# Eight experts over a shared weight stream: a smaller token form, and a scatter over whole row tiles

## The reference, cut to what matters

```python
def _swiglu(h, wg, wu, wd):
    return (jax.nn.silu(h @ wg) * (h @ wu)) @ wd

def _moe(h, router_w, router_b, wg, wu, wd):
    logits = (h @ router_w + router_b).astype(jnp.float32)
    top_v, top_i = lax.top_k(logits, MOE_TOPK)          # MOE_TOPK = 2, N_EXPERTS = 8
    top_w = jax.nn.softmax(top_v, axis=-1)
    gates = jnp.sum(top_w[..., None] * jax.nn.one_hot(top_i, N_EXPERTS, dtype=jnp.float32), axis=-2)
    out = jnp.zeros_like(h)
    for e in range(N_EXPERTS):
        out = out + gates[..., e:e + 1] * _swiglu(h, wg[e], wu[e], wd[e])
    return out
```

## Time and profile before

| | before |
|---|---|
| median of 3 runs | 2109.98 us (2108.65 to 2113.43) |
| profiled execution, its own time | 2107.95 us |
| its span | 2106.2 us |
| TensorE busy, share of the span | 1964.2 us, 93% |
| LDWEIGHTS busy | 1400.2 us, 66% |
| VectorE / ScalarE / GpSimd busy | 508.5 / 276.1 / 363.9 us |
| mean granted TensorE clock | 0.965 |
| chain of work that ended last | TensorE 83%, DMA 8%, VectorE 4% |
| read from HBM | 531.08 MB, mean 253 GB/s |
| one issue of expert weights | 1024.0 KB |
| GB/s in the 40 slices of the span, slices 21 to 40 | 307 393 392 393 351 394 394 395 394 393 394 302 240 240 280 371 395 325 187 22 |

### The profile page before, as it was taken

The page is one execution under the profiler, slowest core; times in us unless marked ns, Lnnn a source line. Parts: engine busy times, 40 slices in busy tenths (PEclk is TensorE's granted clock), DMA queues, the critical chain, the costliest instruction groups (busy, mean ns, idle before and its releaser), DMA issues.

```text
span 2106.2 us, 27964 instructions
## 1 busy us (share of the span) xinstructions
PE 1964.2 (93%) x11330; PEld 1400.2 (66%) x11331; DVE 508.5 (24%) x1165; ACT 276.1 (13%) x518; POOL 363.9 (17%) x215
## 2 busy tenths in 40 slices
PE   2999999989999999999899899998888999998998
PEld 2888788867776888888765555554435877654444
DVE  6293754110001291533220101110101100100002
ACT  1202312010001203412010001000000000101002
POOL 1706750069995000000000000000000000000000
PEclk8899999989999899999989899999999999999998
DMA  9999863268686789733589999999999866799950
GB/s 270 228 183 182 204 187 115 72 221 283 234 288 136 131 147 142 123 121 120 190 307 393 392 393 351 394 394 395 394 393 394 302 240 240 280 371 395 325 187 22
DMA packets 287088, 533.82 MB, mean 253 GB/s; under 512 B 12496, under 2 KB 125696, under 8 KB 286976
## 3 DMA queue, kind: packets, MB, share of 16 engines
q1 hardware_dynamic: 271232, 489.72, 73.6%
q0 software_dynamic: 10880, 41.95, 5.7%
q10 hardware_dynamic: 4864, 0.50, 0.2%
HBM read 531.08 MB, written 1.05 MB: 253 GB/s over the span
## 4 chain that ended last, share of the span: by engine, by line
PE 83%; DMA 8%; DVE 4%; issue 2%; ACT 2%; SPq 1%; POOL 1%; ACTq 0%; DVEq 0%
PE ps L654 20%; PE ps L988 16%; PE ps L1023 9%; PE ps L717 7%; PE ps L726 7%; PE ps L1052 6%; PE ps L737 4%; DMA ring<-in_moe_w_up 4%; PE ps L1068 3%; PE ps L947 2%; PE ps L964 2%; DMA xc<-in_moe_w_down 1%; DMA proj<-in_ada_w 1%; DMA proj<-in_moe_w_up 1%; PE ps L1008 1%
## 5 line engine op out<-in xcount | busy, mean ns | idle before, releaser
L654 PE MATMUL ps<-hT,ring 128*128 128x256 f32 x2048 | 454.6, 383 | 0.0
L654 PEld LDWEIGHTS ps<-hT,ring 128*128 128x128 f32 x2048 | 391.0, 192 | 56.1 <-issue 2.9
L988 PE MATMUL ps<-ring,proj 128*64 128x256 f32 (+2 forms) x1768 | 205.5, 369 | 15.1 <-DMA ring<-in_moe_w_gate 7.9
L567 POOL TENSOR_TENSOR aring<-aring,ccol 128x2048 f32<-128x2048 f32 x40 | 144.7, 3618 | 232.2 <-ACT hT L1163 136.6
L988 PEld LDWEIGHTS ps<-ring,proj 128*64 128x64 f32 (+2 forms) x1768 | 119.5, 133 | 94.6 <-issue 45.1
L1713 DVE TENSOR_TENSOR proj<-proj,ps 128x256 f32<-128x256 f32 (+2 forms) x49 | 23.4, 478 | 648.4 <-PE ps L988 648.4
L726 PE MATMUL ps<-hT,ring 128*128 128x256 f32 x704 | 158.9, 388 | 4.0 <-ACT hT L1163 4.0
L726 PEld LDWEIGHTS ps<-hT,ring 128*128 128x128 f32 x704 | 136.6, 195 | 23.5 <-issue 4.4
L573 POOL TENSOR_TENSOR aring<-aring 128x1024 f32<-128x1024 f32 x80 | 149.0, 1862 | 6.3
L1283 ACT ACTIVATE proj<-ps 128x256 f32<-128x256 f32 (+2 forms) x49 | 21.1, 430 | 622.9 <-PE ps L988 622.9
L1023 PE MATMUL ps<-ring,proj 128*64 128x512 f32 (+2 forms) x360 | 88.3, 608 | 7.9 <-DMA ring<-in_moe_w_down 4.9
(11 more groups left out here) (293 smaller groups left out, 2094.3 us busy)
## 6 DMA issues: line engine op xcount, KB each, us to landing
ring<-in_w_in SPq DMA_DIRECT2D x64, 1024.0 KB, 12.7
ring<-in_moe_w_up SPq DMA_DIRECT2D x56, 1024.0 KB, 14.0
ring<-in_moe_w_gate SPq DMA_DIRECT2D x48, 1024.0 KB, 14.0
aring<-in_ada_w POOLq DMA_DIRECT2D x40, 1024.0 KB, 8.7
ring<-in_moe_w_down SPq DMA_DIRECT2D x40, 1024.0 KB, 13.8
aring<-in_moe_w_gate SPq DMA_DIRECT2D x32, 1024.0 KB, 13.0
extra<-in_moe_w_up SPq DMA_DIRECT2D x16, 1024.0 KB, 14.7
proj<-in_moe_w_down SPq DMA_DIRECT2D x16, 1024.0 KB, 13.7
```

Source lines behind the costliest of these rows:

```text
L567: last = g.tensor_tensor(w, w, ccol[:, :].unsqueeze(2).broadcast_to([P, KT, 256]), ALU.mult)
L654: last = mm(ps[:, n % 2, j * SEQ:(j + 1) * SEQ], wide(s)[:, k, j * P:(j + 1) * P], hT[:, k, :], start=(k == 0), stop=(k == KT - 1))
L988: last = mm(ps[rows * c:rows * (c + 1), bank, 4 * t0:4 * (t0 + rows)], xg[:, 4 * h + k, t0:t0 + rows], w[:, k, 4 * rows * c:4 * rows * (c ...
```

## The change

- `SIZES` gets a sixth, smallest size of 32 (`QUARTER`). `token_blocks(32)` is one block of 32 tokens, which the code of the body already knows: four column tiles. E0, E3 and E6 (24, 30 and 20 tokens) now take this body; the others take the ones they took.
- `by_size` goes, `by_tiles` takes its place: one comparison, 128 or 256 rows. `scatter` uses whole row tiles of 128.
- `ysb` must then hold numbers in the rows that have no token: VectorE sets them to zero (`empty_rows`) in the step g = 1, behind the last `merge` of the expert before. It is one or two memsets of 32 or 64 partitions x 1024; none for the sizes 128 and 256.

```diff
-SIZES = (HALF, 96, 128, 160, 256)
+SIZES = (QUARTER, HALF, 96, 128, 160, 256)
...
-        def by_size(eng, count, body):
-
-            def at(i):
-                if i == len(SIZES) - 1:
-                    body(SIZES[i])
-                    return
-                with eng.If(count <= SIZES[i]):
-                    body(SIZES[i])
-                with eng.Else():
-                    at(i + 1)
-                    eng.nop()
-            at(0)
+        def by_tiles(eng, count, body):
+
+            with eng.If(count <= P):
+                body(P)
+            with eng.Else():
+                body(SEQ)
...
                     for st in range(slot_tiles):
-                        rows = min(P, n - st * P)
-                        last = mm(ps[:, 6 + (m + 1) % 2, 0:SEQ], ysb[0:rows, st, m * P:(m + 1) * P],
-                                  pgT[0:rows, st, :], start=(st == 0), stop=(st == slot_tiles - 1))
+                        last = mm(ps[:, 6 + (m + 1) % 2, 0:SEQ], ysb[:, st, m * P:(m + 1) * P], pgT[:, st, :], start=(st == 0), stop=(st == slot_tiles - 1))
...
                     pe.wait_ge(ye_s, e + 1)
-                    by_size(pe, before, lambda slots: scatter(slots, e * PER + CF0 + C1 - 1))
+                    by_tiles(pe, before, lambda slots: scatter(slots, e * PER + CF0 + C1 - 1))
...
                         if g == 1:
                             merge_before()
+                            empty_rows(n)
                             after = count_after(dve, e)
...
+                def empty_rows(n):
+                    tile, first = (n - 1) // P, (n - 1) % P + 1
+                    while first < P:
+                        rows = HALF if first == HALF else QUARTER
+                        v.memset(ysb[first:first + rows, tile, :], 0.0)
+                        first += rows
```

More of the change, by code:

```diff
@@ L1100, in prepare @@
                     pe.wait_ge(p_s, e + 2)
-                    with pe.If(after <= P):
-                        gather(e * PER + CF0 + C1 + KT, P)
-                    with pe.Else():
-                        gather(e * PER + CF0 + C1 + KT, SEQ)
+                    by_tiles(pe, after, lambda slots: gather(e * PER + CF0 + C1 + KT, slots))
                 return rows_stationary(n) if n <= P else weights_stationary(n)
@@ L1110, in _ @@
             pe.wait_ge(ye_s, EXPERTS + 1)
-            by_size(pe, last_count, lambda slots: scatter(slots, PER * EXPERTS + CF0 + C1 - 1))
+            by_tiles(pe, last_count, lambda slots: scatter(slots, PER * EXPERTS + CF0 + C1 - 1))
             norm_sums(2 * DEPTH)
@@ L1743, in prepared @@
                     v.tensor_copy(pgT[:, 0:st, :], ps[:, 6, 0:st * SEQ].rearrange("p (a b) -> p a b", a=st)).then_inc(cf_s, 1)
-                    with dve.If(after <= P):
-                        tokens(P)
-                    with dve.Else():
-                        tokens(SEQ)
+                    by_tiles(dve, after, tokens)
                 def tokens(width):
```

## The result

The changed kernel took **2117.93 us** (median of 8 runs, 2114.84 to 2119.02); the kernel before, in runs between them on the same chip, 2114.18 (8 runs, 2108.65 to 2118.02). The ratio is **1.0035, with a 95% interval of 1.0019 to 1.0050**: a little slower, where 2087 and a gain of 1% were forecast, and outside the range of 2080 to 2100. The profiled execution took 2116.28 us (before 2107.95), its span is 2114.6.

A forecast was written before the change was run, and what follows sets the result against it. The weight stream bounds up to E4's end, then TensorE through the last three experts. Terms -7 - 1.7 - 8 - 1.7 - 4.35 = -22.8 take the profiled 2107.95 to 2085.2, median 2087 us; range 2080 to 2100.

The forecast's parts named there:

- That jump costs E2 about 3.8 us by E5's row: Entry into the body for 64, no longer behind the ladder: a jump of about 3.8 us, with nothing lost.
- term E: Entry into E7's body: shifted code removes one of two pauses, -4.35 us (bounds 0 and +4.35).
- Term A: E0 to E4, up to the stream's delivery of unit 210: earlier restart and fewer stream stalls, -7 us (bounds -8 and -2).
- E1 stays near the edge: Within E0 to E4: the 67-token expert barely stops filling the slots, so -7 us was taken from 7.8.
- If E3 weren't there, the 3.8 would be on the path: Jump of 3.8 us into the body for 64: hidden because the next expert has 57 us of work in 112 us of stream.
- The sign named in the prediction: End of the 67-token expert: a stream still at 356 GB/s there would show Term A wrong.
- Terms B and D: Scatters in the 153-token expert and E7: no lower clock on down records behind them, -1.7 us each (0 to -2).
- Term C: E6: the weight stream decides instead of TensorE, ending about 1905, -8 us (bounds -4 and -10).
- At nothing: Memsets on VectorE: 1.7 us each, at most 3.4, hidden behind other work, so costed at nothing.
- Low clock: Rival: idle TensorE lowers the clock, costing the ends of E0 and E6; +7, 2094 us; chance 0.17.
- The small form starves on its own instructions: Rival: late code or half clock makes the 32-token step 12.8 us in E0 and E6; 2150 us; chance 0.05 (slower).
- Scatter only: Rival: the 32-token step is no shorter than 10.85 us, Term A and Term C fall away; 2102 us; chance 0.06.

The follow-up runs named there:

- E0: Not a run: the kernel's expert with 24 tokens; 89.4 us in the kernel before, 82.1 in the changed kernel.
- E6: Not a run: the kernel's expert with 20 tokens; 91.8 us in the kernel before, 86.4 in the changed kernel.
- E7: Not a run: the kernel's expert with 128 tokens; 169.4 us in the kernel before, 171.2 in the changed kernel.
- E4: Not a run: the kernel's expert with 49 tokens; 114.1 us in the kernel before, 117.5 in the changed kernel.
- without a common head: Changed kernel, but on TensorE a copy of the ladder behind each body branches straight to the next, without the hint: 2104.18 us, ratio 0.9973.
- body for 32 last: Changed kernel with the body for 32 placed behind all other bodies in memory: 2113.66 us, ratio 1.0021 to the kernel before.
- form-only kernel: Kernel before with size 32 added, keeping by_size and without the memsets: 2146.82 us, ratio 1.0188.
- twin body: Changed kernel with the same six sizes and ladder, but the body taken for 32 tokens computes in the form for 64: 2104.05 us, ratio 0.9961.
- the scatter only: Changed kernel without size 32, leaving the scatter over whole row tiles and the memsets: 2095.31 us, ratio 0.9949 to the kernel before.
- the target hinted: Changed kernel with ladder copies behind TensorE's bodies instead of a common head, plus a prefetch hint for the selected next body: 2088.90 us, ratio 0.9908.
- late hint: Changed kernel with TensorE's prefetch hint for the loop's head moved from the body's start to before the next expert's preparation: 2117.50 us, ratio 1.0029.

## Why the prediction was wrong

The forecast was -22.8 us in the profiled execution; it came out 8.3 us longer instead (E7 ends at 2093.3 and not 2083.1, what follows it is 1.8 shorter). The gap of 31.1, section by section: 2.8 in what precedes the experts (unchanged code, so from run to run), 12.8 in E0 to E4 (-7 forecast, +5.8 measured), 6.9 in E5 (-1.7, +5.2), 2.5 in E6 (-8, -5.5), 7.9 in E7 (-6.05, +1.8), and the -1.8 of the tail.

**The step that failed** is the pricing of the entries: "That jump costs E2 about 3.8 us by E5's row", term E's single pause at E7, and no price at all for E1 and E5. Measured were 6.42 us at E2, 11.76 at E7, 11.68 at E1 and 9.75 at E5. Three faults are in it.

It counted only the branch *into* the body for 64 and not the way *out* of the one for 32, over the head, which costs 5.1 to 5.5 us at E1 and E7 by the run without a common head. The length of the body for 32 was in the text only as a shift of the bodies behind it. At E5 the same run shows 5.1 us for the way over the head, and the one with the body for 32 last shows 5.6 (4.11). But the form-only kernel has the same order and 4.98 there, so this one is not understood.

It took the pause for the fetch. What shows as a pause is what is left of it behind the products still queued on TensorE: the last down product takes 3.58 us in the form for 64 and 1.86 in that for 32. Pause and product together are 4.01 + 3.58 = 7.6 us in E7's entry behind the twin body, 6.27 + 1.86 = 8.1 behind the body for 32 without common head, and 11.76 + 1.86 = 13.6 with it. That is an argument from three rows; no run varied the queued work alone, and E2's entry without common head does not fit it (6.24 behind a product of 5.8).

And it left out that a pause costs clock. E1's first 96 records, first in the changed kernel and then with the scatter only:

```profile
1171.45 8.47 PE L980 MATMUL ps<-aring,proj 128*64 128x256 f32 x96 [11.68 <-issue]
```

```profile
1161.81 5.51 PE L980 MATMUL ps<-aring,proj 128*64 128x256 f32 x96
```

The granted clock is 0.63 from 1170 to 1180 us in the first and 1.00 in the second. So E1's entry costs 11.7 + 3.0 us, which is the whole of the difference of 14.8 us between its two columns in the table.

**Term A** (-7, came +5.8). Its first half, E0, came true, and the rest was undone at the entries. E0 ended 82.1 us after its start (forecast 82), E3's silus lie 16 us apart, as the stream allows:

```profile
1459.68 0.28 ACT L1272 ACTIVATE proj<-ps 128x128 f32<-128x128 f32 x1 [15.15 <-PE ps L980]
...
1475.72 0.28 ACT L1272 ACTIVATE proj<-ps 128x128 f32<-128x128 f32 x1 [15.31 <-PE ps L980]
```

But "E1 stays near the edge" needed E1 at 142 us or less; with 11.7 us at its entry it took 145.0, and E2's entry of 6.42 fell on full slots. The stream at that place, 1300 to 1320 us, in the kernel after (columns as in the earlier trace rows, the last is GB/s):

```profile
1300.00:1310.00 10.00, 4.77 (x46) 1.34 (x42) 1.26 (x4) 3.97 (x7) 0.00 (x0) 0.85 0.76 262
1310.00:1320.00 10.00, 8.81 (x70) 5.65 (x72) 0.31 (x1) 0.38 (x1) 0.00 (x0) 0.80 0.44 153
```

and with the scatter only, where E1 took 130.2 us:

```profile
1162.00:1292.20 130.20, 129.35 (x1751) 75.72 (x1747) 12.48 (x29) 9.26 (x17) 0.00 (x0) 1.00 1.04 393
1300.00:1310.00 10.00, 9.85 (x77) 6.10 (x73) 2.01 (x5) 0.75 (x2) 0.00 (x0) 1.00 1.04 396
```

"If E3 weren't there, the 3.8 would be on the path" was the wrong way round: the stream fell to 262 and then 153 GB/s around E2's entry, and E3 and E4, which end with the stream, do not regain that. The sign named in the prediction (E1's end still slow, then A is wrong) was there: 370 GB/s from 1250 to 1305 us. With the scatter only, E0 to E4 take 538.7 us where they took 543.0: that is 4.3 of A's 7, got because E1 itself lost its two pauses and is 11.3 us shorter, and without the form.

**Terms B and D** (-1.7 each) came as forecast where they were costed. (E5 as a whole is only 0.9 us shorter with the scatter only; its first records after the entry pause are slower there, 4.63 us for 4.02.) Down records behind the scatter in E5 and in E7, in order of time, against the 6.40 and 5.10 us of the earlier trace rows:

```profile
1678.60 4.64 PE L1060 MATMUL ps<-ring,proj 128*128 128x512 f32 x24
...
1969.00 3.60 PE L1015 MATMUL ps<-ring,proj 128*128 128x512 f32 x8
```

**Term C** (-8, came -5.5). E6 after, in order of time:

```profile
1847.53 7.17 PE L957 MATMUL ps<-proj 128*128 128x256 f32 x32 [0.53 <-issue]
...
1913.56 1.59 PE L1015 MATMUL ps<-xc,proj 128*32 128x256 f32 x16 [0.54 <-DMA xc<-in_moe_w_down]
...
1915.46 4.68 PE L941 MATMUL ps<-proj 128*128 128x128 f32 x32
```

The stream binds, as said, and what follows the last wait, 1913.56 to 1922.0, is 8.4 us for a forecast of 8.3, with the gather at its old 4.68. The last wait came 77.9 us after E6's start, though, where the forecast had 1905 - 8.3 - 1822.5 = 74.2. Of these 3.7 us about 2 are 385 instead of 394 GB/s over 86 us; the rest, some two thirds of a unit, was not traced. The two-tile scatter, costed at nothing, in fact fell from 10.1 us to 7.17, which is the size of E6's gain in the kernel with the scatter only (88.8 after 91.8).

**Term E** (-4.35) was right and was then overrun. With the scatter only E7 has one pause of 3.99 where it had 4.03 and 4.35, and takes 162.6 us after 169.4: D and E together, 6.05 forecast, 6.8 measured. That E1's pauses of 2.68 and 2.98 went with it speaks for the prediction's border in the code. The prediction did not count them as a gain. In the changed kernel E7's one pause is 11.76.

**At nothing:** the memsets take 0.91 us each, not 1.7, and nobody waits for them.

**The rivals.** *Low clock*: the clock did fall, to a mean of 0.72 in E3 and 0.85 in E0. At the end of E6, where the rival had its price, the gather ran at its old 4.68 us. The price came elsewhere: 3.0 us behind E1's pause, and in the form-only kernel some 8 us in E6's scatter. *The small form starves on its own instructions* had the right sign, for 5 in 100, and the right family of cause in the wrong place: it looked for the loss within a step. There are such pauses (1.15, 1.51 and 1.46 us in E0, 2.08, 1.79 and 1.41 in E6), but most steps keep the stream's 16 us. The loss is at the borders between bodies. *Scatter only* at 2102 undervalued that half (2095.3). The size of the forecast would nearly have been reached with the target hinted (2088.9).

**What stays open:** why a late hint for the head gained nothing while the early one gains 1 to 3.4 us; why the way over the head costs nothing behind the body for 96, the longest, and 5 us behind the one for 32; why E5's entry is 9.75 us in the changed kernel and 4.98 with the form only; what makes up the 4 us that are left in E1 and E7 with the target hinted. Whether the fetch itself is slow because weight packets fill the DMA engines wasn't tried.

## What to carry to other kernels

A new specialised body is not free even where it is the fastest: count its instructions, ask for each transition in the real sequence of sizes which code must come back (the dispatch code as well as the target), and price each, as a first estimate, by the longest entry pause in the trace plus the work queued ahead of it. Here that gives 4.35 + 3.6, about 8 us. Behind 1.9 us of queued work that would be a pause of 6 us for the target alone (6.3 measured) and of 14 where the head is far too (11.7 measured). A form that splits a product into four column tiles has four times the instructions; when a stream of weights bounds the section anyway, the work it saves is worth little and the code it needs is paid in full. Look at what an edit does to the code's layout even where its work is what you are after: half of the standing still in the kernel before went away with the edit to the scatter, which also took unused variants out of every body. And when a change has two halves, measure them apart: here one gained 0.5% and the other lost more.

## What was not expected of the hardware

- Moving one body in memory, with not one instruction more, costs 1% (2127.3 against 2109.2 us): the three entries of E2, E3 and E4 had no pause above 0.6 us while the body stood next to the ladder, and 6.7 to 7.7 us each once it stood far away.
- TensorE also stands still within the body for 32, 1 to 2 us at a time, where the body for 64 shows no such pause. In E0 three of them end between 1096 and 1109 us, and three packets of the instruction queue moved between 1088 and 1111 us; that they are late code is argued from this, not shown.
- The way over the head and the jump to the target cost 11.7 us, the jump alone 6.3, with the same 1.9 us of work queued ahead. A hint for the branch's target, given ahead of the gather and the last product, took 2.2 us off at two entries, 0.7 at a third and all 4.7 at a fourth.
- A pause is followed by slow matmuls: 96 records took 8.47 us behind 11.68 us of standing still (granted clock 0.63) and 5.51 us without it (1.00).
